# Softmax weights of three attentions divided by their sums ahead of the transposes

## The reference

```python
# window attention: 8 heads of 64; 256 context keys and a band of 3 x 128
p = softmax(concatenate([s, s_sink]))[..., :-1]
o = einsum('bkgqs,bskd->bqkgd', p, vals)
...
# latent attention: 8 heads; keys of 96, values of 64; 1280 keys
p = softmax(s)
o = einsum('bhqk,bkhd->bqhd', p, v)
...
# band attention of the second block: 8 heads of 64, causal chunks, bias
p = softmax(where(valid, s + bias, -inf))
return einsum('bhqk,bkhd->bqhd', p, vc)
```

## Time and profile before

| what | us |
|---|---|
| median of three runs | 3348.8 |
| lowest, highest | 3347.59, 3354.26 |
| the profiled execution, timed | 3353.89 |
| its span | 3352.1 |
| TensorE busy in the span | 3150.2 |
| VectorE, ScalarE, GpSimd busy | 1322.8, 780.2, 483.6 |
| window attention, from its first matmul to the next block's | 261.4 to 411.8 |
| latent attention | 500.8 to 812.4 |
| band attention | 1991.4 to 2118.0 |

### The profile page before, as it was taken

One profiled execution on the slowest core, in us unless ns is written; L12 is line 12 of the kernel. 1 busy time (PEld: TensorE's weight loads), 2 busy tenths in 40 slices (PEclk: granted clock), 3 DMA queues, 4 the chain that ended last, 5 costly groups with the idle time before them and its releaser, 6 DMA issues. The chain is left out here.

```text
span 3352.1 us, 35976 instructions
## 1 busy us (share of the span) xinstructions
PE 3150.2 (94%) x14346; PEld 1681.5 (50%) x14346; DVE 1322.8 (39%) x2353; ACT 780.2 (23%) x1548; POOL 483.6 (14%) x389
## 2 busy tenths in 40 slices
PE   7999999999949999599999999999999999998998
PEld 3447756765424444344456657444444444443443
DVE  2216635553351111524322466414625454544233
ACT  3116524443221111312212126211011111111001
POOL 0000000000000100013122200212303232321323
PEclk8999999999979999699999999999999999999999
DMA  7210000003366886601000130012201111113443
GB/s 284 76 51 28 2 4 23 1 1 122 120 251 256 333 338 207 204 33 38 25 27 27 51 132 2 32 38 100 76 38 51 38 51 38 50 38 144 129 129 132
DMA packets 65830, 311.43 MB, mean 93 GB/s; under 512 B 10240, under 2 KB 11777, under 8 KB 51841
## 3 DMA queue, kind: packets, MB, share of 16 engines
q1 hardware_dynamic: 61056, 292.35, 23.3%
q0 software_dynamic: 4608, 16.78, 2.0%
HBM read 272.39 MB, written 36.70 MB: 92 GB/s over the span
## 5 line engine op out<-in xcount | busy, mean ns | idle before, releaser
L2701 PE MATMUL banks<-hT,ffn_ring 128*128 128x512 f32 x528 | 235.9, 596 | 1.1 <-PEq L2401 1.1
L2852 PE MATMUL banks<-down_ring,down_sums 128*128 128x512 f32 x440 | 189.2, 592 | 0.0
L2701 PEld LDWEIGHTS banks<-hT,ffn_ring 128*128 128x128 f32 x528 | 101.0, 192 | 128.6 <-issue 128.5
L329 PE MATMUL banks<-w_in,hT 128*128 128x512 f32 (+1 forms) x384 | 159.2, 572 | 5.0 <-PEq L157 5.0
L2701 PE MATMUL banks<-ffn_row_sums,ffn_w_sums 128*128 128x512 f32 x352 | 158.3, 592 | 1.1 <-DVE ffn_row_sums L2732 1.1
L821 PE MATMUL banks<-kT_b,qT_b 96*128 96x512 f32 (+1 forms) x384 | 158.4, 522 | 0.8 <-PEq L104 0.8
L2742 DVE SCALAR_TENSOR_TENSOR ffn_acc<-ffn_u,s_ffn_taps,ffn_acc 128x1023 f32<-128x1023 f32 x88 | 129.1, 1466 | 67.9 <-ACT ffn_acc L2725 66.4
L853 DVE TENSOR_REDUCE softmax_columns_b<-banks 128x1 f32<-128x1280 f32 x64 | 95.5, 1492 | 143.5 <-PE banks L821 143.5
L2852 PEld LDWEIGHTS banks<-down_ring,down_sums 128*128 128x128 f32 x440 | 83.6, 190 | 105.2 <-issue 103.8
L1600 PE MATMUL banks<-hT,side_ring 128*128 128x512 f32 x256 | 127.5, 618 | 1.3 <-PEq L2216 1.3
L1323 PE MATMUL banks<-expert_wg,expert_xT 128*128 128x512 f32 x256 | 115.2, 603 | 2.4 <-ACT expert_xT L1360 1.7
(11 more groups left out here) (514 smaller groups left out, 5226.7 us busy)
## 6 DMA issues: line engine op xcount, KB each, us to landing
down_ring<-in_w_down SPq DMA_DIRECT2D x132, 256.0 KB, 2.9
expert_wg<-in_w_gate SPq DMA_DIRECT2D x16, 2048.0 KB, 15.3
expert_wu<-in_w_up SPq DMA_DIRECT2D x16, 2048.0 KB, 20.7
expert_wd<-in_w_down SPq DMA_DIRECT2D x16, 2048.0 KB, 8.6
ffn_ring<-in_w_ffn SPq DMA_DIRECT2D x22, 1024.0 KB, 4.8
wmod_slab<-in_w_mod SPq DMA_DIRECT2D x6, 2048.0 KB, 8.0
wmod_ring<-in_w_mod SPq DMA_DIRECT2D x4, 2048.0 KB, 10.7
w_out<-in_w_out SPq DMA_DIRECT2D x4, 2048.0 KB, 8.1
```

The costliest lines, as they stand in the source:

```text
L329: last = nc.tensor.matmul(c.ps[:, base + a:base + b], h[:, q, :], k.w_in[i][:, q, 0:b - a], start=q == 0, stop=q == KD - 1)
L2701: last = nc.tensor.matmul(product(f, m), wt[:, q, :], x[:, q, :], start=q == 0 and m != 2, stop=q == 3, skip_group_check=True)
L2852: last = nc.tensor.matmul(c.bank(4 * (p % 2) + t), stationary[:, P * t:P * t + P], w[s % RING][:, 0, :], start=j == 0, stop=j == N - 1)
```

## The change

In all three attentions `prob` is divided by the sum ahead of the transposes, and the product is only copied out. In `attend_latent` VectorE does it, one multiply of 128x1280 a head, behind a reciprocal a head. In `attend_pairs` VectorE takes the reciprocals (`inverse`) of unit u-1 behind the maximum of unit u, and GpSimd, which gets a loop in these blocks, multiplies head by head, counted by `evened`. The matmul of row scales, the spreading copy and the multiply of the product are gone, and so is their buffer. `prob` has three buffers in the place of two. The transposes wait for `evened` and belong to unit u-2 instead of u-1; the product belongs to unit u-3; so each loop has one slot more. In `attend_latent` the wait for the exponentials of head u-1 stands ahead of the last third of the scores of head u. For the sinks the maximum is taken negated, and two small operations follow instead of three. Some buffers lie at other addresses.

```diff
@@ -586,15 +586,14 @@
...
-                freed.append((scaled, s))
+                freed.append((taken, s))
...
     def product(v):
-        at = BANK * (TURN + use_of_product[v] % 2)
-        return c.ps[:, at:at + P], c.ps[:, at + P:at + 2 * P]
+        return c.bank(TURN + use_of_product[v] % 2, P)
...
@@ -602,7 +601,7 @@
...
-        return prob[:, s % 2, i // pair.tiles, P * (i % pair.tiles):P * (i % pair.tiles) + P]
+        return prob[:, s % 3, i // pair.tiles, P * (i % pair.tiles):P * (i % pair.tiles) + P]
...
@@ -613,7 +612,7 @@
...
-                    pe.wait_ge(exped, 2 * s + 1 + (a + m - 1) // pairs[s].tiles)
+                    pe.wait_ge(evened, 2 * s + 1 + (a + m - 1) // pairs[s].tiles)
...
-            for s in range(-1, n + 1):
-                u = s + 1
+            for s in range(-2, n + 1):
+                u = s + 2
...
                         for e in range(2):
-                            nc.tensor.matmul(out[64 * e:64 * e + 64, :], pairs[v].values[e][j],
+                            last = nc.tensor.matmul(out[64 * e:64 * e + 64, :], pairs[v].values[e][j],
                                              probT[:, v % 2, P * (e * tiles + j):P * (e * tiles + j) + P],
                                              start=j == 0, stop=j == tiles - 1, skip_group_check=True)
-                    pe.wait_ge(rowed, v + 1)
-                    nc.tensor.matmul(rows, wide[:, v % 2, :], k.ident[:, :], start=True, stop=True,
-                                     skip_group_check=True).then_inc(mixed, 1)
+                    last.then_inc(mixed, 1)
                 if 0 <= s < n:
                     turn(s, slice(2, 3))
...
         @block.vector
         def _(dve):
             step = Chain(dve, link)
-            for s in range(-1, n + 1):
-                u = s + 1
+
+            def inverse(v):
+                st = col[:, v % 4]
+                dve.wait_ge(exped, 2 * (v + 1))
+                if pairs[v].sink is not None:
+                    dve.wait_ge(sunk, v + 1)
+                    step(nc.vector.tensor_tensor(st[:, 2, :], st[:, 2, :], st[:, 4, :], ALU.add))
+                nc.vector.reciprocal(st[:, 0, :], st[:, 2, :]).then_inc(inverted, 1)
+
+            for s in range(-2, n + 1):
+                u = s + 2
                 if u < n:
                     pair, st = pairs[u], col[:, u % 4]
                     dve.wait_ge(scored, u + 1)
                     if u >= 4:
-                        dve.wait_ge(scaled, u - 3)
+                        dve.wait_ge(evened, 2 * (u - 3))
                     if pre is None:
-                        step(nc.vector.reduce_max(st[:, 0, :], both(u), AX.X))
-                        step(nc.vector.tensor_tensor(st[:, 0, :], st[:, 0, :], pair.sink, ALU.max))
-                        step(nc.vector.tensor_scalar(st[:, 1, :], st[:, 0, :], -1.0, None, ALU.mult))
-                        nc.vector.tensor_tensor(st[:, 3, :], pair.sink, st[:, 0, :], ALU.subtract).then_inc(negmax, 1)
+                        step(nc.vector.reduce_max(st[:, 0, :], both(u), AX.X, negate=True))
+                        step(nc.vector.scalar_tensor_tensor(st[:, 1, :], pair.sink, -1.0, st[:, 0, :], ALU.mult, ALU.min))
+                        nc.vector.tensor_tensor(st[:, 3, :], pair.sink, st[:, 1, :], ALU.add).then_inc(negmax, 1)
...
-                if 0 <= s < n:
-                    st = col[:, s % 4]
-                    dve.wait_ge(exped, 2 * (s + 1))
-                    if pairs[s].sink is not None:
-                        dve.wait_ge(sunk, s + 1)
-                        step(nc.vector.tensor_tensor(st[:, 2, :], st[:, 2, :], st[:, 4, :], ALU.add))
-                    step(nc.vector.reciprocal(st[:, 0, :], st[:, 2, :]))
-                    if s >= 2:
-                        dve.wait_ge(mixed, s - 1)
-                    nc.vector.tensor_copy(wide[:, s % 2, :].rearrange("p (e d) -> p e d", e=2),
-                                          st[:, 0, :].unsqueeze(2).to_broadcast([P, 2, 64])).then_inc(rowed, 1)
+                    if u:
+                        inverse(u - 1)
+                if u == n:
+                    inverse(n - 1)
                 if s >= 1:
                     v = s - 1
-                    out, rows = product(v)
                     dve.wait_ge(mixed, v + 1)
-                    nc.vector.tensor_copy(pairs[v].out, rows).then_inc(spread, 1)
-                    dve.wait_ge(spread, v + 1)
-                    nc.vector.tensor_tensor(pairs[v].out, pairs[v].out, out, ALU.mult).then_inc(scaled, 1)
+                    nc.vector.tensor_copy(pairs[v].out, product(v)).then_inc(taken, 1)
                 if 0 <= s < n:
                     piece_out(dve, s, 1, nc.vector.tensor_copy, out_dve)
 
+        @block.gpsimd
+        def _(pool):
+            for s, pair in enumerate(pairs):
+                m = P * pair.tiles
+                pool.wait_ge(inverted, s + 1)
+                for e in range(2):
+                    nc.gpsimd.tensor_tensor(prob[:, s % 3, e, 0:m], prob[:, s % 3, e, 0:m], col[:, s % 4, 0, e:e + 1].to_broadcast([P, m]),
+                                            ALU.mult).then_inc(evened, 1)
...
         def _(act):
-            for s in range(-1, n):
+            for s in range(-2, n):
                 if s >= 0:
                     piece_out(act, s, 0, lambda o, i: nc.scalar.activation(o, i, ACT.Identity), out_act)
-                u = s + 1
+                u = s + 2
                 if u < n:
                     pair, st = pairs[u], col[:, u % 4]
                     act.wait_ge(negmax, u + 1)
                     if pair.sink is not None:
                         nc.scalar.activation(st[:, 4, :], st[:, 3, :], ACT.Exp).then_inc(sunk, 1)
-                    if u >= 2:
-                        act.wait_ge(turned, of_pair[u - 2][-1] + 1)
+                    if u >= 3:
+                        act.wait_ge(turned, of_pair[u - 3][-1] + 1)
                     m = P * pair.tiles
                     for e in range(2):
-                        nc.scalar.activation(prob[:, u % 2, e, 0:m], scores(u, e, 0, m) if pre is None else pre[:, u % 2, e, 0:m],
+                        nc.scalar.activation(prob[:, u % 3, e, 0:m], scores(u, e, 0, m) if pre is None else pre[:, u % 2, e, 0:m],
...
@@ -763,8 +766,7 @@
...
     def product(p):
-        at = 7 * BANK
-        return c.ps[:, at:at + P], c.ps[:, at + P:at + 2 * P]
+        return c.bank(7, P)
...
@@ -794,20 +796,18 @@
...
-                    last = nc.tensor.transpose(turn_bank(u, i)[:, P * j:P * j + P], prob[:, u % 2, P * (a + j):P * (a + j) + P],
+                    last = nc.tensor.transpose(turn_bank(u, i)[:, P * j:P * j + P], prob[:, u % 3, P * (a + j):P * (a + j) + P],
...
-                out, rows = product(p)
...
                     if p:
-                        pe.wait_ge(scaled, p)
-                    pe.wait_ge(rowed, p + 1)
-                    nc.tensor.matmul(rows, wide[:, p % 2, :], k.ident[:, :], start=True, stop=True, skip_group_check=True)
+                        pe.wait_ge(taken, p)
...
-            for s in range(-1, n + 2):
-                u = s + 1
+            for s in range(-2, n + 2):
+                u = s + 2
                 if u < n:
                     if u >= 2:
                         pe.wait_ge(exped, u - 1)
                     score(u, 0)
                 if 0 <= s < n:
-                    pe.wait_ge(exped, s + 1)
+                    pe.wait_ge(evened, s + 1)
                     turn(s, 0)
                 if u < n:
+                    if u:
+                        pe.wait_ge(exped, u)
                     score(u, 1).then_inc(scored, 1)
...
         @block.vector
         def _(dve):
             step = Chain(dve, link)
-            for s in range(-1, n + 2):
-                u = s + 1
+            for s in range(-2, n + 2):
+                u = s + 2
+                if 0 <= u - 1 < n:
+                    st = col[:, (u - 1) // 2 % 4, :, (u - 1) % 2:(u - 1) % 2 + 1]
+                    dve.wait_ge(exped, u)
+                    step(nc.vector.reciprocal(st[:, 2, :], st[:, 1, :]))
+                    nc.vector.tensor_scalar(prob[:, (u - 1) % 3, :], prob[:, (u - 1) % 3, :], st[:, 2, :], None, ALU.mult).then_inc(evened, 1)
                 if u < n:
                     st = col[:, (u // 2) % 4]
                     dve.wait_ge(scored, u + 1)
-                    if u >= 8 and u % 2 == 0:
-                        dve.wait_ge(scaled, u // 2 - 3)
                     nc.vector.reduce_max(st[:, 0, u % 2:u % 2 + 1], scores(u), AX.X, negate=True).then_inc(negmax, 1)
...
-                    if s % 2 == 1:
-                        p = s // 2
-                        st = col[:, p % 4]
-                        dve.wait_ge(exped, s + 1)
-                        step(nc.vector.reciprocal(st[:, 2, :], st[:, 1, :]))
-                        if p >= 2:
-                            dve.wait_ge(mixed, p - 1)
```

(46 more changed lines are left out.)

1 line of the change is left out of this document (removed).

## The result

The changed kernel takes 3329.8 us (median of four runs, 3327.97 to 3330.07), the kernel before 3351.5 beside it (3347.59 to 3354.43): the ratio is 0.9939, 95% interval 0.9926 to 0.9951. Faster by 0.6%; forecast were 3332 and "faster". The median fell by 21.7 us where 17 were forecast; that the time lies so near to 3332 owes something to the kernel before, whose median is 3351.5 here and was 3348.8 when the forecast was made. The span fell by 24.7 us, from 3352.1 to 3327.4.

What follows compares the result with a forecast made beforehand. TensorE's instruction stream was taken to bound the three attentions. Latent -5.8, window -5.3 and band some -6 make -17 us, from a median of 3348.8 to say 3332; range 3322 to 3350.

Steps and rivals of the forecast that it cites:

- What bounds: All three attentions: TensorE's instruction stream sets the pace, so what counts is what is taken from it.
- Price of the row-scale matmul: All three attentions: removing it saves 0.21 us a pair, 6.7 us a stage, 20 us in all.
- rival (4): Window and band: gaps behind the row-scale matmul close too (5 us), short band slots lose all waits (3); 3324, chance 0.14.
- Latent multiply: Latent: VectorE's added 128x1280 multiply takes at most 0.94 us; its loop of 4.14 fits the 4.65 slot.
- Rival (3): Latent: the loop closes on VectorE at 4.7 us, the stage gains nothing; time 3338, chance 0.08.
- Fill and drain: Latent: one slot deeper, the end some 1.6 us longer and the beginning some 0.7 shorter, net 0.9 us.
- GpSimd's price: Window and band: each GpSimd multiply of up to 128x640 by a column takes 1.25 us.
- The first rival (1.53): Window and band: the spread column brings no speed, 1.53 us a GpSimd instruction; gain 10, time 3339, chance 0.18.
- the second (2.1): Window and band: VectorE holds GpSimd, 2.1 us an instruction; slower than before, time 3362, chance 0.14.
- Window: Window: five-tile slots at 4.58 us, GpSimd hidden up to 1.43 an instruction; -6.7 + 1.4 = -5.3 us.
- Band: Band: five-tile slots at 4.39 us, GpSimd hidden up to 1.54 an instruction; -6.7 - 1 + 1.4, some -6 us.
- the treatment of the short slots as one lump of 1 us: Band: GpSimd's way exceeds TensorE's work in short slots, but waits for exponentials go; counted as 1 us gained.

Runs made afterwards that it cites:

- GpSimd on two columns: The changed kernel with GpSimd multiplying only the first 2 columns of each head in window and band, most of the division left out; 3313.7 us.
- heads split: The changed kernel with VectorE multiplying head 1 of each pair while GpSimd does head 0, in window and band; 3326.1 us.

## Why the prediction was right, point by point

- **What bounds.** Right: putting the matmul back undoes the gain, but for 0.8 us of the band stage.
- **Price of the row-scale matmul.** Low in two stages. Taken was 0.21 us a pair, 6.7 a stage. Put back it costs 9.2, 7.3 and 7.8, or 0.29, 0.23 and 0.24; taken out at the old depth it was worth 10.8, 7.5 and 11.7, or 0.34, 0.23 and 0.37. The window's slots gave 0.27 where a third piece follows and 0.42 where none does, so the gaps closed as rival (4) had it, and 0.21, the gap between two loads of weights, was too low in every slot. The latent price, read from two slots that differ by this matmul alone, was the best of the three.
- **Latent multiply.** 0.886 us for at most 0.94; a loop of 3.97 for 4.14; slots of 4.64. Rival (3) fell with that. Fill and drain cost 7.3 - 6.3 = 1.0 us for 0.9.
- **GpSimd's price.** Taken 1.25 us; measured

```profile
L727 POOL TENSOR_TENSOR prob<-prob,softmax_columns x64: 1038/1252/1256, 266.0 to 398.2; 128x640 f32<-128x640 f32 x48, 128x512 f32<-128x512 f32 x16
```

  The first rival (1.53) and the second (2.1) fell on this row. By the Trainium skill (GPSIMD Engine Reference, opening and section 3) 1.5 us was estimated; the measurement decides against it for this form.
- **Window.** Slot forecast 4.58, measured 4.52. All but the matmul cost 9.2 - 7.5 = 1.7 us for 1.4 by the run that puts it back, and 3.3 by the run that takes it out at the old depth; the second counts against the change the slots in which a wait for GpSimd took the matmul's place.
- **Band.** That -8.6 was measured for -6 is the sum of three errors, which in part cancel by luck. Removal gained 11.7 us where 6.7 were counted. The deeper loop gained 3.5 (of which up to 1.7, by the rounds rather 0.6, may be the clock) where fill and drain were to cost 1.4 and short slots to gain 1. And GpSimd costs 6.6, where it was counted free. The end did get 1.3 us longer (10.9 from the last negation on for 9.6); what the sum left out is the beginning, where the first seven intervals between negations of the maximum (one a unit) add up to 20.0 us for 25.0 before, since the short first slots no longer wait for the exponentials (21.0 with the matmul put back, 23.3 at the old depth without it). GpSimd's cost shows in every round, 28.55 us for 27.04 with GpSimd on two columns, most of it between the negations of a round's first two five-tile units: 4.44 us apart for 3.44. Rounds of eight were forecast at 28.3. The step that failed is the treatment of the short slots as one lump of 1 us.
- **Sum.** -17 forecast; -22.4 measured in the three stages. Another 0.7 of the span lies ahead of the window stage, and 1.6 in the block behind the band, where eight matmuls took 5.23 us before

```profile
2124.85 5.23 PE L2482 MATMUL banks<-gate_rows,gate_sums 128*128 128x512 f32 x8 [3.14 <-DVE gate_rows L2543]
...
2126.00:2130.00 4.00, 4.00 (x9) 1.70 (x8) 4.00 (x2) 0.00 (x0) 3.10 (x1) 0.75 0.02 4
```

  at a mean granted clock of 0.75 (a part of these 4 us at the 1.2 GHz level, the rest at 2.4), and after

```profile
2101.68 3.67 PE L2473 MATMUL banks<-gate_rows,gate_sums 128*128 128x512 f32 x8 [3.14 <-DVE gate_rows L2534]
...
2103.00:2107.00 4.00, 4.00 (x11) 1.80 (x10) 4.00 (x2) 0.00 (x0) 2.92 (x1) 1.00 0.01 4
```

  at 1.00, with the same idle time of 3.14 us ahead. This block's matmuls up to the first on `oaT` take 195.7 to 198.6 us over all runs, in no order with the edits; it isn't counted to the change.

## What to carry to other kernels

Where one engine's stream sets the pace, an instruction taken out of it is worth its place in the steady slot (read it from two slots that differ by it), and what replaces it on a slower engine is free up to a slack that a loop over two slots gives; try to spend that slack on purpose before counting on it. Irregular slots (short units, a long one behind short ones) need a sum of their own. Before work goes to GpSimd, ask if VectorE has room: here it had, and GpSimd was the reason why the three stages got 22 us shorter and not 30. Where a difference rests on a stage's first slots, compare the granted clock there too.

## What the runs showed of the hardware

Not expected was that VectorE is held by GpSimd. With the heads split, durations (min/median/max) of VectorE's and GpSimd's multiply:

```profile
L691 DVE TENSOR_SCALAR prob<-prob,softmax_columns x32: 1365/1645/1648, 265.6 to 396.9; 128x640 f32<-128x640 f32 x24, 128x512 f32<-128x512 f32 x8
...
L732 POOL TENSOR_TENSOR prob<-prob,softmax_columns x32: 1039/1252/1254, 265.7 to 396.9; 128x640 f32<-128x640 f32 x24, 128x512 f32<-128x512 f32 x8
```

A VectorE multiply of 128x640 from SBUF to SBUF takes 1.65 us beside GpSimd's and 0.55 without it; GpSimd's takes 1.25 either way. The Trainium skill (SBUF — State Buffer, SBUF: two separate sides) says that the two engines share a port pair as an exclusive lock for the whole instruction, also for a VectorE operation in a two-port mode, and that the loser is blocked entirely. The trace agrees: VectorE's multiply ends 0.35 us behind GpSimd's. From 0.886 us for 1280 elements and 0.548 for 640 its elements take an estimated 0.53 ns each, 0.34 us for 640, with a fixed part of 0.21; so nearly all of them came after GpSimd's end. At 128 elements it ends 0.08 us behind, at 512 0.28, which fits too. Which mode it ran in no run shows. By the same sentence the engine that starts first wins; here VectorE's multiply is recorded 0.04 us ahead of GpSimd's (338.28, 338.32), in all 64 units of the two stages, and lost. The records don't show which of the two reached the ports first. The maximum, which reads PSUM, is not held: L695 has a mean of 1424 ns in the changed kernel, where it overlaps GpSimd's multiplies in part (340.19 to 341.68 beside 338.49 to 340.95).

```profile
L695 DVE TENSOR_REDUCE softmax_columns<-banks 128x2 f32<-128x1280 f32 (+1 forms) x32 | 45.6, 1424 | 36.0 <-PE banks L642 36.0
...
L699 DVE TENSOR_REDUCE softmax_columns<-banks 128x2 f32<-128x1280 f32 (+1 forms) x32 | 45.6, 1425 | 22.0 <-PE banks L642 22.0
```

The second line is of the kernel with both heads on VectorE, where GpSimd is silent.

GpSimd's multiply by a column spread over the row costs 1.252 us for 640 and 1.039 for 512: 1.67 ns an element and a fixed part of 0.19 us, the latter borne out by 0.196 for two columns.
